# Expert results added to DRAM rows by an accumulating scatter, and block-only score squares at two recurrence levels

## The reference, cut to what matters

```python
A = jnp.einsum('bthk,btshk,bshk->bhts', q, decay, k)      # decay = exp(b_t - b_s) where s <= t, else 0
...
yp = yp + merge_groups(...)                                # attention | recurrence, output projection, residual
g_sel = jnp.argmax(g_logits, axis=-1)                      # top 1 of 4 groups
top_v, top_i = lax.top_k(e_logits, TOP_K)                  # top 2 of the group's 8 experts
gates = p_group * jax.nn.softmax(top_v, axis=-1)
ys = lax.map(run, (xs, blk_exp)).reshape(R, t.shape[1])    # per block of 128 rows: (silu(x wg) * (x wu)) wd
ys = ys * row_gate[:, None].astype(ys.dtype)
moe = jax.ops.segment_sum(ys, row_tok, num_segments=N + 1)[:N]
y_prompt = rmsnorm(yp + moe, final_w)
```

## Time and profile before

| | us |
|---|---|
| median of 3 runs | 3017.4 (3015.2 to 3017.56) |
| the profiled execution's own time | 3016.05 |
| its span in the profile | 3014.2 |
| TensorE busy | 2756.1 (91%) |
| VectorE busy | 1478.0 (49%) |
| ScalarE busy | 1010.5 (34%) |
| GpSimd busy | 444.7 (15%) |
| mean granted TensorE clock | 0.960 |

### The profile page before, as it was taken

How to read it: one execution, slowest core, us unless ns; L and a number is a source line. 1 busy time by engine, 2 the same in 40 slices (tenths; PEclk the granted TensorE clock), 3 DMA queues, 4 the chain that set the end, 5 groups by cost and what they waited for, 6 DMA issues and landing times. The chain is left out here.

```text
span 3014.2 us, 40049 instructions
## 1 busy us (share of the span) xinstructions
PE 2756.1 (91%) x13121; PEld 1746.3 (58%) x13122; DVE 1478.0 (49%) x2674; ACT 1010.5 (34%) x2181; POOL 444.7 (15%) x684
## 2 busy tenths in 40 slices
PE   8999999999999949999779998699999999999960
PEld 6777777777777647777655554344444444444420
DVE  2556555655656558888725555223232322323227
ACT  2333333334333327777535553000101001010118
POOL 2111111111111113333200111000101101010100
PEclk9999999999999979999989998799999999999985
DMA  6000010001000060000142221777646467575658
GB/s 238 32 32 25 24 41 32 24 24 38 35 24 24 30 223 8 15 8 15 38 162 96 90 84 46 260 291 288 255 181 249 182 236 296 205 288 213 228 196 300
DMA packets 167710, 382.85 MB, mean 127 GB/s; under 512 B 13378, under 2 KB 30530, under 8 KB 165456
## 3 DMA queue, kind: packets, MB, share of 16 engines
q1 hardware_dynamic: 153328, 333.76, 30.6%
q0 software_dynamic: 14304, 48.08, 4.2%
HBM read 310.73 MB, written 71.08 MB: 127 GB/s over the span
## 5 line engine op out<-in xcount | busy, mean ns | idle before, releaser
L659 PE MATMUL z_psum<-w_in_sb,hT 128*128 128x512 f32 x1088 | 480.5, 592 | 0.0
L653 PE MATMUL z_psum<-hT,w_in_sb 128*128 128x128 f32 x3264 | 374.8, 276 | 0.8 <-ACT hT L326 0.8
L653 PEld LDWEIGHTS z_psum<-hT,w_in_sb 128*128 128x128 f32 x3264 | 370.7, 193 | 1.7 <-ACT hT L326 1.2
L1919 PE MATMUL gate_psum<-w_gate_sb,block_rows_T 128*128 x720 | 323.2, 602 | 13.0 <-SPq L1751 12.0
L659 PEld LDWEIGHTS z_psum<-w_in_sb,hT 128*128 128x128 f32 x1088 | 200.5, 190 | 221.0 <-issue 221.0
L1943 PE MATMUL down_psum<-w_down_sb,hidden_T 128*128 x720 | 323.7, 592 | 0.9 <-ACT hidden_T L1825 0.9
L1923 PE MATMUL up_psum<-w_up_sb,block_rows_T 128*128 x720 | 316.3, 592 | 0.0
L1628 PE MATMUL y_psum<-w_out_sb,mix_T 128*128 128x512 f32 x544 | 242.9, 600 | 0.9 <-DVE mix_T L1485 0.9
L1923 PEld LDWEIGHTS up_psum<-w_up_sb,block_rows_T 128*128 128x128 f32 x720 | 136.8, 190 | 172.2 <-issue 172.2
L1919 PEld LDWEIGHTS gate_psum<-w_gate_sb,block_rows_T 128*128 128x128 f32 x720 | 135.5, 193 | 168.8 <-issue 168.8
L1943 PEld LDWEIGHTS down_psum<-w_down_sb,hidden_T 128*128 128x128 f32 x720 | 133.3, 190 | 151.8 <-issue 151.8
(11 more groups left out here) (316 smaller groups left out, 3510.5 us busy)
## 6 DMA issues: line engine op xcount, KB each, us to landing
w_gate_sb<-in_w_e_gate SPq DMA_DIRECT2D x32, 2048.0 KB, 8.4
w_up_sb<-in_w_e_up SPq DMA_DIRECT2D x32, 2048.0 KB, 14.6
w_down_sb<-in_w_e_down SPq DMA_DIRECT2D x32, 2048.0 KB, 18.1
expert_rows<-scratch_moe SPq DMA_DIRECT2D x17, 1024.0 KB, 8.4
w_in_sb<-in_w_in SPq DMA_DIRECT2D x7, 2048.0 KB, 19.1
scratch_z<-z_ring SPq DMA_DIRECT2D x34, 256.0 KB, 2.0
scratch_h<-h SPq DMA_DIRECT2D x17, 512.0 KB, 2.6
x_tile<-in_x_prompt SPq DMA_DIRECT2D x16, 512.0 KB, 3.6
```

The source lines that it names most:

```text
L653: mm = pe.matmul(out[:, hd * P:(hd + 1) * P], w[:, c, col:col + P], hT[:, u, c, :], start=(c == 0), stop=(c == DC - 1))
L659: mm = pe.matmul(out[:, :], hT[:, u, c, :], w[:, c, g * HW:(g + 1) * HW], start=(c == 0), stop=(c == DC - 1))
L1919: mm = pe.matmul(gps[:, :], xT[:, u, c, :], part(wg, slot, c), start=(c == 0), stop=(c == DC - 1))
```

## The change

Two parts.

**Recurrence levels.** For m = 64 and m = 32, TensorE forms only the wanted squares: at m = 64 one 64x64 square per head (four matmuls of 64 weight columns and 64 moving columns), at m = 32 two 32x32 squares per head (eight matmuls), each at the partitions where it belongs. VectorE copies only them: one plain copy of 64 partitions by 256 values, two of 32 partitions by 128. The smaller levels are as before.

**Experts' sum.** `y` is stored per tile to a DRAM tensor `acc` by SyncE's queue in `mix_and_route` and kept in SBUF for two tiles only. The queue table's entries become pairs of float32 (token, gate); the gate is scattered with the token, and both come back per block (`tok_all`, `gate_all`). The gate is applied where `out` is copied from PSUM. The scatter adds `out` to the token's row of `acc` inside the DMA. `finish` then loads one row per token (512 KB a tile, all 17 loads issued at once), takes the logarithm and exponential for batches of four tiles, and has four output buffers.

```diff
-PAD_ROWS = P // 2
+PAD_ROWS = P
...
+def blocks_of(m):
+
+    return [(s0, s0 + m) for s0 in range(0, P, 2 * m)]
...
             def merge(t, pos, m):
...
+                if m >= P // 4:
+                    for s0, t0 in blocks_of(m):
+                        c = slice(t0, t0 + m)
+                        ins = nc.vector.tensor_copy(heads(A[s0:s0 + m, :])[:, :, c], heads(lps[pos % 2][s0:s0 + m, :])[:, :, c])
+                    ins.then_inc(cp_ok, 1)
+                    return
...
             def level(t, u, pos):
...
+                m = levels(t)[pos][1]
+                if m >= P // 4:
+                    for hd in range(HEADS):
+                        for s0, t0 in blocks_of(m):
+                            row_c, col_c = (slice(hd * P + a, hd * P + a + m) for a in (s0, t0))
+                            mm = pe.matmul(lps[pos % 2][s0:s0 + m, col_c], left[:, row_c], right[:, col_c], start=True, stop=True)
+                    mm.then_inc(lv_ps, 1)
+                    return
...
# mix_and_route, SyncE, per tile
                 if there(t - 1):
+                    sp.wait_ge(y_ok, 2 * t)
+                    sp.dma_start(row(acc, t - 1), y[:, 1 - u, :]).then_inc(y_out, 16)
                     sp.wait_ge(h_ok, t)
                     sp.dma_start(row(h2, t - 1), h[:, 1 - u, :]).then_inc(h_out, 16)
...
# its end
             sp.dma_start(dr["h2"][TILES * P:TILES * P + PAD_ROWS], zero[:, :]).then_inc(h_out, 16)
+            sp.dma_start(dr["acc"][TILES * P:TILES * P + PAD_ROWS], zero[:, :]).then_inc(y_out, 16)
             sp.wait_ge(h_out, 16 * (TILES + 1))
+            sp.wait_ge(y_out, 16 * (TILES + 1))
...
# GpSimd: table set up, its scatter and its fetch
+            pool.memset(init[:, :, :, 1], 0.0)
+            chain.after(pool.iota(init[:, :, :, 0], [[0, 5], [1, P]], base=TILES * P, channel_multiplier=0, **kw))
...
-                            in_=slot_now[:, u, c:c + 1], in_offset=None).then_inc(sc_out, 16)
+                            in_=entry[:, u, c, :], in_offset=None).then_inc(sc_out, 16)
...
# VectorE
             def residual(t, u, half):
...
+                if half == 0:
+                    wait(dve, y_out, 16 * t - 16)
+                tt(y[:, u, c], yps[:, half, :], x[:, u, c], ALU.add).then_inc(y_ok, 1)
...
-                cp(slot_now[:, u, :], slot[:, bass.ds(t, 1), :].rearrange("p o c -> p (o c)")).then_inc(pos_ok, 1)
+                cp(entry[:, u, :, 1], gates[:, :])
+                cp(entry[:, u, :, 0], token[:, bass.ds(t, 1)].to_broadcast([P, 2])).then_inc(pos_ok, 1)
...
-            cp(blk[:, :], blk_rows[:, :]).then_inc(blk_ok, 1)
+            cp(blk[:, :, :], blk_rows[:, :, :].rearrange("p r o -> p o r")).then_inc(blk_ok, 1)
             dve.wait_ge(blk_ps, 1)
-            chain.after(cp(slot_all[:, :], yps[:, 0, 0:P]))
-
-            ts(tok_all[:, :], slot_all[:, :], 0.5, -0.25, ALU.mult, ALU.add)
+            cp(tok_all[:, :], yps[:, 0, 0:P])
+            cp(gate_all[:, :], yps[:, 0, P:2 * P])
...
# TensorE
-            pe.transpose(yps[:, 0, 0:P], blk[:, :], ident[:, :]).then_inc(blk_ps, 1)
+            pe.transpose(yps[:, 0, 0:P], blk[:, 0, :], ident[:, :])
+            pe.transpose(yps[:, 0, P:2 * P], blk[:, 1, :], ident[:, :]).then_inc(blk_ps, 1)
...
# experts
-                pool.indirect_dma_start(out=dr["moe"], out_offset=bass.IndirectOffsetOnAxis(ap=slots[:, u:u + 1], axis=0),
-                                        in_=out[:, u, :], in_offset=None).then_inc(o_out, 16)
+                pool.indirect_dma_start(out=dr["acc"], out_offset=bass.IndirectOffsetOnAxis(ap=slots[:, u:u + 1], axis=0),
+                                        in_=out[:, u, :], in_offset=None, compute_op=ALU.add).then_inc(o_out, 16)
...
-                nc.scalar.copy(out[:, u, 0:HW], dps[:, 0, :]).then_inc(d_act, 1)
+                nc.scalar.activation(out[:, u, 0:HW], dps[:, 0, :], ACT.Copy, scale=gate_all[:, bass.ds(b, 1)]).then_inc(d_act, 1)
...
-                cp(out[:, u, HW:D], dps[:, 1, :]).then_inc(d_dve, 1)
+                ts(out[:, u, HW:D], dps[:, 1, :], gate_all[:, bass.ds(b, 1)], None, ALU.mult).then_inc(d_dve, 1)
...
# finish
+    BATCHES = [(0, 4), (4, 8), (8, 12), (12, 16), (16, TILES)]
...
+            sp.dma_start(y[:, 0, :], acc[0]).then_inc(y_in[0], 16)
             sp.dma_start(fw[:, :], dr["final_w"].to_broadcast([P, D])).then_inc(fw_in, 16)
+            for t in range(1, TILES):
+                sp.dma_start(y[:, t, :], acc[t]).then_inc(y_in[t], 16)
             for t in range(TILES):
                 sp.wait_ge(o_ok, t + 1)
                 dst = yp[t] if t < NT else dr["y_sample"].rearrange("b t d -> (b t) d")
+                sp.dma_start(dst, o[:, t % 4, :]).then_inc(o_out[t % 4], 16)
...
+            for t0, t1 in BATCHES:
+                for t in range(t0, t1):
+                    act.wait_ge(y_in[t], 16)
+                    ins = nc.scalar.activation(junk[:, :], y[:, t, :], ACT.Square, accum_out=st[:, 0, t:t + 1])
+                    chain.after(ins)
+                chain.after(nc.scalar.activation(st[:, 1, t0:t1], st[:, 0, t0:t1], ACT.Ln, scale=1.0 / D, bias=consts["eps"][:, 0:1]))
+                nc.scalar.activation(st[:, 2, t0:t1], st[:, 1, t0:t1], ACT.Exp, scale=-0.5).then_inc(r_ok, 1)
...
+            for n, (t0, t1) in enumerate(BATCHES):
+                dve.wait_ge(r_ok, n + 1)
+                for t in range(t0, t1):
+                    dve.wait_ge(y_in[t], 16)
+                    wait(dve, o_out[t % 4], 16 * (t // 4))
+                    stt(out=o[:, t % 4, :], in0=y[:, t, :], scalar=st[:, 2, t:t + 1], in1=fw[:, :], op0=ALU.mult, op1=ALU.mult).then_inc(o_ok, 1)
```

More of the change, by code:

```diff
@@ L1365, in _ @@
             kw = dict(allow_small_or_imprecise_dtypes=True)
-            chain.after(pool.iota(init[:, :, :], [[0, 5], [1, P]], base=2 * TILES * P, channel_multiplier=0))
-            pool.dma_start(dr["table"].rearrange("(a b) r o -> a (b r o)", b=5), init[:, :, :].rearrange("a b r -> a (b r)")).then_inc(tab_out, 16)
-            pool.iota(slot[:, :, :], [[2 * P, TILES], [1, 2]], base=0, channel_multiplier=2)
+            pool.memset(init[:, :, :, 1], 0.0)
+            chain.after(pool.iota(init[:, :, :, 0], [[0, 5], [1, P]], base=TILES * P, channel_multiplier=0, **kw))
+            pool.dma_start(dr["table"].rearrange("(a b) r o -> a (b r o)", b=5), init[:, :, :, :].rearrange("a b r o -> a (b r o)")).then_inc(tab_out, 16)
+            pool.iota(token[:, :], [[P, TILES]], base=0, channel_multiplier=1, **kw)
             pool.iota(e_of[:, :], [[1, N_EXP]], base=0, channel_multiplier=0, **kw)
@@ L1404, in _ @@
             pool.wait_ge(lst_ok, 1)
-            pool.indirect_dma_start(out=blk_rows[:, :], out_offset=None, in_=dr["table"].rearrange("a r o -> a (r o)"),
+            pool.indirect_dma_start(out=blk_rows[:, :, :].rearrange("p r o -> p (r o)"), out_offset=None,
+                                    in_=dr["table"].rearrange("a r o -> a (r o)"),
                                     in_offset=bass.IndirectOffsetOnAxis(ap=blk_at[:, :], axis=0)).then_inc(blk_in, 16)
@@ L1430, in step @@
                     wait(act, h_ok, t - 1)
-                    chain.after(nc.scalar.activation(junk[:, :], y[:, bass.ds(t - 1, 1), :].rearrange("p o d -> p (o d)"),
-                                                     ACT.Square, accum_out=st[:, 0:1]))
+                    chain.after(nc.scalar.activation(junk[:, :], y[:, 1 - u, :], ACT.Square, accum_out=st[:, 0:1]))
                     chain.after(nc.scalar.activation(st[:, 1:2], st[:, 0:1], ACT.Ln, scale=1.0 / D, bias=eps))
@@ L1480, in residual @@
                 dve.wait_ge(y_ps, 2 * t + half + 1)
-                tt(y[:, bass.ds(t, 1), c].rearrange("p o n -> p (o n)"), yps[:, half, :], x[:, u, c], ALU.add).then_inc(y_ok, 1)
+                if half == 0:
+                    wait(dve, y_out, 16 * t - 16)
+                tt(y[:, u, c], yps[:, half, :], x[:, u, c], ALU.add).then_inc(y_ok, 1)
             def copy_mT(t, u):
@@ L1516, in gate @@
                 chain.after(ts(sel[:, 0:1], rt[:, 3:4], 1.0, rt[:, 1:2], ALU.add, ALU.mult))
-                g = gates[:, bass.ds(t, 1), :].rearrange("p o c -> p (o c)")
-                chain.after(nc.vector.reciprocal(g[:, 0:1], sel[:, 0:1]))
-                chain.after(tt(g[:, 1:2], g[:, 0:1], rt[:, 3:4], ALU.mult))
+                chain.after(nc.vector.reciprocal(gates[:, 0:1], sel[:, 0:1]))
+                chain.after(tt(gates[:, 1:2], gates[:, 0:1], rt[:, 3:4], ALU.mult))
             def positions(t, u):
@@ L1965, in _, with finish @@
             down(n * 2, 0)
-def finish(nc, dr, consts, keep):
-    y, gates = keep["y"], keep["gates"]
+def finish(nc, dr, consts):
+    BATCHES = [(0, 4), (4, 8), (8, 12), (12, 16), (16, TILES)]
     with ExitStack() as ctx:
@@ L1987, in _ @@
         def _(sp):
-            def load(t):
-                wait(sp, y_ok, t - 3)
-                sp.dma_start(e[:, t % 4, :, :].rearrange("p c d -> p (c d)"), moe[t]).then_inc(e_in[t % 4], 16)
```

(15 more changed lines are left out.)

67 lines of the change are left out of this document (26 added, 41 removed).

## The result

| | before | after |
|---|---|---|
| median, us | 3016.4 (4 runs) | 2974.99 (2972.91 to 2978.9, 4 runs) |
| ratio | | 0.9863, 95% interval 0.9851 to 0.9875 |
| span of the profiled execution, us | 3014.2 | 2971.2 |
| mean granted clock | 0.960 | 0.966 |

What follows compares the result with a forecast made beforehand. TensorE was taken as nearly always busy in recurrence and experts, ScalarE and DMA as loaded in finish. Finish -40, levels -13, mix +1, last scatter +2, added reading +1 give -49: 2968 us from a median of 3017.4, range 2959 to 2977.

Steps and rivals of the forecast that it cites:

- the levels: Recurrence, m = 64 and 32: narrow squares and a shorter wait save 0.8 us a tile, 13 us over 16 tiles.
- the added reading: Experts: the accumulating scatter reads 23.6 MB more beside the weight loads; 1 us more, bounds 0 and 15.
- the queueing of the first stores behind the loads: Finish: loads done near 26 us, stores after; VectorE's second batch waits for buffers until 27.5, the end at 49 us.
- the 46.6 of ScalarE's count: Finish: ScalarE's batches of 7.9 us, then VectorE's last multiplies and the tail, would end the stage at 46.6 us.
- The rival of a stage bound by DMA at 0.306: Finish: at the earlier mean DMA rate the stage takes 60 us, 2979 us in all; chance 0.09.
- most of this wait goes: 0.3 a tile: Recurrence: two short copies replace the masked merge of 0.73 us, so TensorE's wait behind level 2 shrinks by 0.3 us.
- The rival that gave narrow instructions a price of 0.111 us: Recurrence: narrow instructions have their own floor, so the levels cost 9.5 us instead of saving 13: 2990 us; chance 0.11.
- the rival of late weight loads: Experts: weight loads come late beside the added DMA traffic, 15 us more, 2983 us; chance 0.05.
- The last scatter: Experts: its landing is exposed before the stage's barrier, 0 to 3.4 us more, taken as 2 more.
- The rival of the scatter's chain: Experts: landings past 20.3 us set the block period; at 23 us, +121 us, 3089 us; chance of slower 0.10.
- The bound of twice the time: Experts: an accumulating scatter's landing takes from nothing more to twice the 7.8 us median, 15.6 us, under the 20.3 hidden.
- the store's wait: Mix and route: VectorE's new wait for the store's buffer has about a period of cover; whole stage 1 us more.

Runs made afterwards that it cites:

- e6: The changed kernel with finish loading each tile's rows a second time into an unread buffer, 27.3 MB instead of 18.4, batches kept: 2999.04 us.
- e7: The changed kernel with full squares and a masked merge at m = 64, narrow squares at m = 32 only: 2983.91 us in one run.
- e9: The changed kernel with VectorE's gate chain just before the forget gates, level 3's operand ahead of level 2's merge, its exponential earlier on ScalarE: 2966.03 us.
- e4: The changed kernel with a plain scatter into the same rows, without the add in the DMA, so its output is incomplete: 2968.67 us.
- e8: The kernel before, with finish's logarithm and exponential in batches of four tiles and its loads issued further ahead: 3015.0 us, ratio 0.9992.

## Why the prediction was right, and where it was off

The time lies 7 us above the forecast and 2 us inside the upper end of its own range. Two terms were off, the levels and the added reading, and both in the same direction, so no error hid another in the sum.

**Finish: right, and by its own steps.** 48.8 us against 49. The fourth tile was put at 8.5 us (its own terms, 2.5 + 5 x 0.52 / 0.4, give 9.0) and landed at 9.6; the first store buffer was put at 27.5 and came free at 27.6; the queueing of the first stores behind the loads, which made the difference between the 46.6 of ScalarE's count and 49, is the 12.2 us store of the chain. That the end is met to 0.2 us is partly luck: the multiplies behind it came every 1.24 us, not 1.35, and from the start of the last one to the end it took 6.2 us, not 5.2. The DMA engines moved some 0.41 MB/us, about the 0.4 estimated (27.27 MB in e6's 70.7 us are 0.386 with the ends). The rival of a stage bound by DMA at 0.306 is out: that mean had the other engines' pace in it.

**Levels: right in direction, 0.4 us a tile where 0.8 was put, 8.3 us of stage where 13 was.** The step that failed is "most of this wait goes: 0.3 a tile". It took the wait for L493 as the merge's length. It was the end of a serial chain on VectorE that starts at the copy of the projection's second group, and the merge ahead of it lost only 0.15 us of busy time (two copies cost 0.29 each) and 0.03 from start to start. Every tenth that TensorE gained between that point and the wait was given back in it, beyond what VectorE gained: e7 shows 0.37 turning into 0.11, e9 shows the whole 0.6 us a tile that lay behind the wait. So the wait's price did not fall by 0.3, it rose from 0.55 to 0.61. The instructions themselves were sized about right: 0.60 and 0.37 against twice 0.89 are 0.81 less, of which some 0.35 goes to the changes of shape (0.10 ahead of the first, 0.20 between the two, about 0.05 behind the second), and 0.46 is left where 0.5 was put (the table of periods says the same: 60.48 to 60.02). The wait was also worth nearly twice what its row says.

The Trainium skill's limit of about 62 ns per matmul with hardware decode off (TensorE: Matmul & The Clock Gate, "Wait — 56ns, not 53.3ns?"), weighed in the prediction, does not bind here: sixteen instructions of the level of m = 32 take 0.37 us, 23 ns each. The other floor that the prediction took from there, about 25 ns, isn't kept either: the first and the last of the sixteen start 0.25 us apart, 17 ns each. The rival that gave narrow instructions a price of 0.111 us is out.

**Experts: right in sum for this pair of profiles, not in its terms.** The stage grew by 4.1 us where 3 was put; over all profiles the kernels with the add lie nearly 8 above those without. The added reading was put at 1 us and cost about 6 (e4), within its bounds of 0 and 15; so the rival of late weight loads was at work, with a third of its price. The last scatter was put at 2 and costs nothing. Its landing is at least 2.7 us later (6.0 against 3.3 at the shortest), but the stage's end is held by something else: the trace has a drain instruction of GpSimd behind the loop, of 7.50 us in the kernel before and in e4 and 4.35 in the changed one, which ends 10.8 to 11.0 us after the last scatter's issue in all three. That the drain alone sets the end was read, not tried. The rival of the scatter's chain needed a landing of 21.4 us; the longest was 10.3. The copy to `out` is not the first to wait for the landing, as the prediction has it: in the earlier trace rows GpSimd's own copy of the slots waits already, but there GpSimd idles for 13 and 18 us ahead of its scatters, so this costs nothing. The bound of twice the time was right for the transfer at its shortest (3.3 to 6.0) and generous for the median (7.8 to 9.2). The Trainium skill's sentence that an add costs its two reads (Collectives: The Full Stack, "The bandwidth ceiling: the fold count and why AG ≠ RS ≠ AR") agrees with that first pair, 1.8 times, though not with the median, 1.2 times.

**Mix and route: right.** 0.1 us where 1 was put, within its bounds; the store's wait and the table's second column cost nothing that the stage's length shows.

## What to carry to other kernels

Where a stage has several engines near each other's pace, count each one's time after the edit before giving any of them a gain: finish had three bounds between 71 and 85 us, and batching the table loads alone (e8) brought 4 us in the stage and nothing that could be measured in the whole. A short wait in a trace is the end of a chain; before pricing it away, follow it back to where the chain starts and ask what else stands in it, and whether the instruction waited for could simply go first. Narrow squares pay on TensorE what is left after the changes of the array's shape: 0.37 us a tile at m = 32, only 0.09 at m = 64.

## What the runs showed of the hardware

- Going from 128 weight columns to 64 or 32 and back costs about 0.1 us each time, 0.05 behind the level of m = 32. It shows in the neighbouring full-width groups (6.87 us becomes 6.97 and 7.07), and the first weight load of the new shape starts with its matmul instead of 0.43 us ahead of it. That this load is the cost was read, not tried.
- Sixteen instructions of 32 by 32 took 0.37 us, but eight of 64 by 64 took 0.60: 0.023 and 0.075 each, the changes of shape inside the groups included. Those of m = 32 go in turn to two different quarters of the output partitions.
- A wait of TensorE counted as 0.35 us cost 0.6 in the period, since the eight instructions behind it took 1.00 us instead of 0.89 and from the start of the transposes to its own start it was 1.39 us instead of 0.88.
- An indirect scatter that adds occupies GpSimd for 1.59 us instead of 1.00, and its DMA queue for 6.7% instead of 4.3% (e4) of the engines' time at equal bytes.
- Two copies from PSUM of 32 partitions by 128 values took 0.58 us, one of 64 by 256 took 0.41: here the count of VectorE's instructions mattered more than the values in each.
